# Retention heads: the decay moved onto v and into the group norm's epsilon, two transposes per unit

## The reference, cut to what matters

```python
decay = where(rel >= 0, exp(rel * log_gamma), 0)          # rel = i - j inside a chunk
xi    = exp((pos + 1) * log_gamma);  zeta = exp((c - 1 - pos) * log_gamma)
inner = einsum('bnihd,bnjhd->bnhij', qc, kc) * decay      # scores of a chunk
inner = einsum('bnhij,bnjhe->bnihe', inner, vc)
new_state = einsum('bjhd,bjhe->bhde', k_i * zeta, v_i) + chunk_decay * state
cross = einsum('bnihd,nbhde->bnihe', qc, prev_states) * xi
o = inner + cross
o = (o - mean(o)) * rsqrt(var(o) + 1e-6)                  # over the 64 of a head
return silu(g) * (o * gn_w + gn_b)
```

## Time and profile before

| | |
|---|---|
| time, median of 3 runs (lowest, highest) | 2803.08 us (2801.38, 2803.82) |
| the profiled execution's own time | 2803.51 us |
| its span in the profile | 2801.7 us |
| PE busy, share of the span | 2616.1 us, 93% |
| DVE, ACT, POOL busy | 1545.0, 1106.1, 1043.1 us |
| first layer: retention loop to the projection's first matmul | 565.0 to 660.1 us |
| second layer: the same | 1950.8 to 2046.7 us |

### The profile page before, as it was taken

How to read it: one execution, slowest core, us unless ns; L and a number is a source line. 1 busy time by engine, 2 the same in 40 slices (tenths; PEclk the granted TensorE clock), 3 DMA queues, 4 the chain that set the end, 5 groups by cost and what they waited for, 6 DMA issues and landing times. The chain is left out here.

```text
span 2801.7 us, 43296 instructions
## 1 busy us (share of the span) xinstructions
PE 2616.1 (93%) x13164; PEld 2250.8 (80%) x13164; DVE 1545.0 (55%) x2993; ACT 1106.1 (39%) x2567; POOL 1043.1 (37%) x1271
## 2 busy tenths in 40 slices
PE   6999888989999999999989997988898999999997
PEld 5999777867778888888879996777787888888886
DVE  4666453373464555477657765433725544544785
ACT  4444453262432222244444444433515323223444
POOL 3454422173144444301034554221911554452012
PEclk9999999958999999999989999998599999999999
DMA  5110101021323332473331101012122223335633
GB/s 172 28 57 19 40 5 36 29 91 60 102 72 109 105 109 89 149 291 99 99 105 31 34 19 37 6 36 71 49 83 79 94 94 109 109 105 198 234 98 121
DMA packets 238653, 243.09 MB, mean 87 GB/s; under 512 B 27904, under 2 KB 170752, under 8 KB 238464
## 3 DMA queue, kind: packets, MB, share of 16 engines
q1 hardware_dynamic: 238464, 240.83, 26.5%
HBM read 173.14 MB, written 67.63 MB: 86 GB/s over the span
## 5 line engine op out<-in xcount | busy, mean ns | idle before, releaser
L2256 POOL TENSOR_TENSOR fw_a_lo<-fw_a_raw,fw_a_hi 128x512 fp32r<-128x512 f32 x132 | 179.2, 1358 | 527.2 <-DVE fw_s_raw L1859 527.2
L2256 POOL TENSOR_TENSOR fw_s_lo<-fw_s_raw,fw_s_hi 128x512 fp32r<-128x512 f32 x176 | 230.0, 1319 | 50.8 <-ACT fw_s_hi L1377 50.8
L693 PE MATMUL banks<-ht_hi,da_hi 128*128 128x512 f32 x496 | 192.9, 389 | 0.0
L693 PE MATMUL banks<-ht_lo,da_hi 128*128 128x512 f32 x496 | 192.9, 389 | 0.0
L693 PE MATMUL banks<-ht_hi,da_lo 128*128 128x512 f32 x496 | 192.9, 389 | 0.0
L693 PE MATMUL banks<-w_diff_hi,ht_hi 128*128 128x384 f32 x512 | 180.3, 352 | 6.4 <-DVE ht_lo L1563 4.4
L1193 ACT ACTIVATE pt_hi<-banks 128x512 fp32r<-128x512 f32 (+2 forms) x144 | 67.4, 502 | 298.1 <-PE banks L796 297.9
L693 PE MATMUL banks<-w_diff_hi,ht_lo 128*128 128x384 f32 x512 | 172.4, 337 | 0.0
L693 PE MATMUL banks<-w_diff_lo,ht_hi 128*128 128x384 f32 x512 | 172.1, 336 | 0.0
L2104 POOL TENSOR_TENSOR qk_rot<-rope_a,rope_b 128x512 f32<-128x512 f32 x64 | 82.7, 1293 | 208.2 <-DVE rope_b L1592 208.2
L1620 DVE TENSOR_REDUCE stats<-banks 128x1 f32<-128x1024 f32 (+3 forms) x192 | 138.8, 749 | 38.0 <-PE banks L890 33.0
(11 more groups left out here) (354 smaller groups left out, 7781.2 us busy)
## 6 DMA issues: line engine op xcount, KB each, us to landing
da_raw<-act_scratch SPq DMA_DIRECT2D x154, 256.0 KB, 2.6
fw_a_raw<-in_w_gate_dram SPq DMA_DIRECT2D x88, 256.0 KB, 3.0
act_scratch<-act_s SPq DMA_DIRECT2D x66, 256.0 KB, 3.0
w_diff_raw<-in_w_in_dram SPq DMA_DIRECT2D x24, 512.0 KB, 5.8
fw_a<-in_w_up_dram SPq DMA_DIRECT2D x44, 256.0 KB, 3.2
fw_a_raw<-in_w_up_dram SPq DMA_DIRECT2D x44, 256.0 KB, 2.9
act_scratch<-act_zero SPq DMA_DIRECT2D x44, 256.0 KB, 2.4
act_scratch<-act_one SPq DMA_DIRECT2D x44, 256.0 KB, 2.8
```

The lines of the kernel that those rows point to most:

```text
L693: mm = pe.matmul(bank, lhsT, rhs, start=first and i == 0, stop=last and i == len(pairs) - 1, skip_group_check=resumes)
L2256: pool.tensor_tensor(w[1][:], w[2][:], w[0][:].bitcast(F32), ALU.subtract).then_inc(S["f_lo"], 1)
```

## The change

In a chunk, the decay between output row i and column j is gamma^(i+1) times gamma^-(j+1). The column factor gamma^-(j+1), with the scale of 64^-0.5, is now multiplied onto v, by one more DVE instruction before each rotation. The row factor gamma^(i+1) is left out: it scales a whole row of the output, and the group norm takes it out again if its epsilon is multiplied by gamma^(-2(i+1)), a table of two columns per pair. So:

- the scores are multiplied by a triangle of ones and zeros, 128x128, instead of the `decay` table of 128x512; its DMA carries 64 KB instead of 256 KB;
- neither q nor k is scaled: `ret_scaled` (four ACT instructions per unit) and the third transpose go, and `rt_hi` and `rt_lo` are 256 wide instead of 384;
- the state is multiplied by the chunk's decay when it is rounded: ACT with a scale, and the low part by a DVE scalar_tensor_tensor (`ret_state_low`) instead of POOL's subtraction;
- the normalisation goes from DVE to ACT (`ret_normed`, two instructions Identity with scale and bias), and DVE only forms the bias `r_nb` (`ret_offset`);
- POOL adds the epsilon from the table, a tensor_tensor instead of a tensor_scalar;
- on ACT `rt_hi` stands ahead of `rk_hi`, and the loop runs two steps further for the last two `ret_normed`, ahead of `weights(CH_OUT + 1)`.

```diff
+    age = (pos[:, None] + 1.0) * log_gamma[None, :].astype(np.float64)
     for p in range(RET_PAIRS):
-        c[:, C_XZ + 4 * p:C_XZ + 4 * p + 2] = xi[:, 2 * p:2 * p + 2]
-        c[:, C_XZ + 4 * p + 2:C_XZ + 4 * p + 4] = zeta[:, 2 * p:2 * p + 2]
+        c[:, C_XZ + 4 * p:C_XZ + 4 * p + 2] = (np.exp(-age) * RET_DIM ** -0.5)[:, 2 * p:2 * p + 2]
+        c[:, C_XZ + 4 * p + 2:C_XZ + 4 * p + 4] = (GN_EPS * np.exp(-2.0 * age))[:, 2 * p:2 * p + 2]
...
-                arrives(decay[:], decay_dram.rearrange("p (a n) -> p a n", a=RET_PAIRS), "ret_in")
+                arrives(causal[:], causal_dram, "ret_in")
...
-                    pe.wait_ge(S["r_xz"], L * PER["r_xz"] + n + 1)
+                    pe.wait_ge(S["rope_sum"], L * PER["rope_sum"] + ROPE_RET + n + 1)
...
-                    pe.transpose(bank[:, tokens(2)], r_xzt[n % 3][:, 0:2, :].rearrange("p a d -> p (a d)"), ident[:])\
...
-                    for i in range(4):
-                        st = act.activation(r_xzt[n % 3][:, i, :], r_rot[n][:, i, :], ACT.Copy, scale=xz[:, n // T, i:i + 1])
...
+                def ret_normed(n):
+                    b = n % 2
+                    act.wait_ge(S["r_nb"], L * PER["r_nb"] + n + 1)
...
+                    for j in range(2):
+                        st = act.activation(r_norm[b][:, 64 * j:64 * j + 64], r_sum[b][:, j, :], ACT.Identity,
+                                            bias=r_nb[:, b, j:j + 1], scale=r_rs[:, b, j:j + 1])
...
-                for n in range(1, RET_UNITS + 2):
+                for n in range(1, RET_UNITS + 4):
                     if 1 <= n <= RET_UNITS:
+                        ret_high(n - 1)
                         ret_high_k(n - 1)
-                        ret_high(n - 1)
-                    if n >= 2:
+                    if 2 <= n < RET_UNITS + 2:
                         ret_inner(n - 2)
+                    if n >= 4:
+                        ret_normed(n - 4)
                     if n + 1 < RET_UNITS:
                         ret_gate_and_v(n + 1)
-                        ret_scaled(n + 1)
                     if 2 <= n < 2 + PARTS:
                         weights(CH_OUT, [n - 2])
                 weights(CH_OUT + 1)
...
+                    v = r_z[n][:, 2 * P:3 * P].rearrange("p (j d) -> p j d", j=2)
+                    dve.tensor_tensor(v, v, xz[:, n // T, 0:2].unsqueeze(2).to_broadcast([P, 2, RET_DIM]), ALU.mult)
                     rotate(r_z[n][:, 0:2 * P], r_ab[0], r_ab[1], n % T).then_inc(S["rope_ab"], 1)
...
+                def ret_state_low(n):
...
+                        dve.scalar_tensor_tensor(r_st2[i % 3][:, 1, :], r_st[:], cd[:, p:p + 1], r_st2[i % 3][:, 0, :].bitcast(F32),
+                                                 ALU.mult, ALU.subtract).then_inc(S["r_stlo"], 1)
...
+                def ret_offset(n):
...
+                    dve.scalar_tensor_tensor(r_nb[:, b, :], mv[:, b, :, 0], -1.0, r_rs[:, b, :], ALU.mult, ALU.mult).then_inc(S["r_nb"], 1)
```

More of the change, by code:

```diff
@@ L359, in hybrid_block_kernel @@
     sin_m = keep("sin_m", [P, T, 2, 16])
-    stats = keep("stats", [P, 148])
+    stats = keep("stats", [P, 152])
     taken = [0]
@@ L401, in hybrid_block_kernel @@
     r_ms = small(2, 2)
+    r_nb = small(2, 2)
     minus_half = small(4)
-    assert taken[0] <= 148, taken[0]
+    assert taken[0] <= 152, taken[0]
     assert base + at[0] <= nc.sbuf_usable_end, at[0] - CREG
@@ L1319, in ret_high @@
                         act.wait_ge(S["ro_done"], L * PER["ro_done"] + n - 2)
-                    act.activation(rt_hi[n % 3][:].rearrange("p b n -> p (b n)"), banks[:, TR_BANKS[r % 2], 0:3 * P], ACT.Copy)\
+                    act.activation(rt_hi[n % 3][:].rearrange("p b n -> p (b n)"), banks[:, TR_BANKS[r % 2], 0:2 * P], ACT.Copy)\
                         .then_inc(S["tr_hi"], 1)
@@ L1776, in ret_inner @@
                         dve.wait_ge(S["r_atlo"], L * PER["r_atlo"] + n)
-                    dve.tensor_tensor(r_at[:].rearrange("p (j n) -> p j n", j=2), banks[:, 0:2, 0:P], decay[:, p, :].rearrange("p (j n) -> p j n", j=2), ALU.mult).then_inc(S["r_at"], 1)
+                    dve.tensor_tensor(r_at[:].rearrange("p (j n) -> p j n", j=2), banks[:, 0:2, 0:P], causal[:].unsqueeze(1).to_broadcast([P, 2, P]), ALU.mult).then_inc(S["r_at"], 1)
                     if n % T < T - 1:
@@ L1811, in ret_normed @@
                     if n >= 2:
-                        dve.wait_ge(S["r_gw"], L * PER["r_gw"] + n - 1)
-                    for j in range(2):
-                        st = dve.tensor_scalar(r_norm[b][:, 64 * j:64 * j + 64], r_sum[b][:, j, :],
-                                               mv[:, b, j, 0:1], r_rs[:, b, j:j + 1], ALU.subtract, ALU.mult)
-                    st.then_inc(S["r_on"], 1)
+                        dve.wait_ge(S["r_on"], L * PER["r_on"] + n - 1)
+                    dve.scalar_tensor_tensor(r_nb[:, b, :], mv[:, b, :, 0], -1.0, r_rs[:, b, :], ALU.mult, ALU.mult).then_inc(S["r_nb"], 1)
                 for a in MLA_STEPS:
@@ L2204, in ret_low_k @@
                     pool.wait_ge(S["r_kzhi"], L * PER["r_kzhi"] + n + 1)
-                    pool.tensor_tensor(rk_lo[b][:], r_xzt[n % 3][:, 2:4, :].rearrange("p a d -> p (a d)"), rk_hi[b][:].bitcast(F32), ALU.subtract)\
+                    pool.tensor_tensor(rk_lo[b][:], r_rot[n][:, 2:4, :].rearrange("p a d -> p (a d)"), rk_hi[b][:].bitcast(F32), ALU.subtract)\
                         .then_inc(S["r_kzlo"], 1)
@@ L2220, in ret_root @@
                     pool.sem_inc(S["passed"], 1)
-                    pool.tensor_scalar(r_ms[:, b, :], mv[:, b, :, 1], GN_EPS, None, ALU.add).then_inc(S["r_ms"], 1)
+                    pool.tensor_tensor(r_ms[:, b, :], mv[:, b, :, 1], xz[:, n // T, 2:4], ALU.add).then_inc(S["r_ms"], 1)
                     pool.wait_ge(S["r_ms"], L * PER["r_ms"] + n + 1)
```

62 lines of the change are left out of this document (25 added, 37 removed).

## The result

| | before | changed |
|---|---|---|
| time, median | 2803.45 us | 2823.74 us (2822.96 to 2825.42) |
| span of the profiled execution | 2801.7 us | 2823.6 us |
| first `r_at` to first `ht_lo`, first layer | 77.29 us | 85.91 us |
| the same, second layer | 77.29 us | 85.93 us |

The ratio is 1.0071, with a 95% interval of 1.0057 to 1.0084: 20.3 us slower. The forecast was +6.7, and 2816 as the upper end of its range. The direction was right, the size a third of what came. The ratios in this document leave out one slow execution, of e5 (4904.45 us, one of ten).

The account below looks back on a forecast made before the run. The retention was taken to have no single bound but five stretches with different last waits; -0.3 - 1.5 + 4.7 + 0.2 + 0.25 = +3.35 us a layer, twice +6.7, gave 2809.8 us, range 2803 to 2816.

Parts of the forecast that it names:

- The start: First r_at, waiting for gn_b's DMA: the smaller table ahead of it gains 0.3 us a layer, between 0 and 1.2.
- The steps with w_o: Retention steps with POOL's four w_o_lo: later starts 6.2 us apart instead of 6.47, 1.5 us a layer gained (0.3 to 2.5).
- rival 1: DVE's scalar_tensor_tensor is not held by POOL, so r_nb goes through at once: net +1.5 a layer, 2806; chance 0.18.
- Rival 3: In the steps with w_o, ACT's waiting r_norm holds rt_hi and scores: steps stay 6.47, no gain, 2813; chance 0.09.
- The later units: Units after the w_o steps: one transpose less on PE, 0.9 us a layer gained of a possible 1.7 (0.2 to 1.7).
- The ring: Root, r_nb, r_norm on ACT, three products, epsilon, root: 3.9 us, or 4.2 with the next low part in the way.
- The last units: Units 14 and 15: two more turns through ACT at 0.3 each, 0.6 us a layer lost (0.4 to 1.2).
- From the last root to `ht_lo`: Retention's end: w_o's four ACT roundings now stand behind the last r_norm, 4.7 us a layer lost (4.5 to 5.0).
- Clock and MLA steps: PE's idle before the refill costs 0.2 us a layer (0 to 2.5); the product on v costs 0.25 at the last rotation.
- rival 2: TensorE's clock does not come back while PE refills its banks: 1.6 us a layer more, 2813; chance 0.12.
- Rival 4: PE's clock rises to 2.4 GHz inside the loop: 6.5 us a layer faster, 2790; chance 0.06.
- The chances: Probabilities given for the measured outcome: slower 0.56, same 0.38, faster 0.06, with about 0.2% as the limit.

Follow-up runs that it names:

- e5: Changed kernel with DVE's sum and statistics of unit n-3 moved ahead of v's and the state's low parts, ACT's order untouched; 2803.5 us, ratio 0.9995.
- e1: Changed kernel with v's copy and the gate of unit n+1 ahead of the normalisation of unit n-4 on ACT; 2808.5 us, ratio 1.0011.
- e3: Changed kernel with the normalisation back as two DVE instructions, no r_nb, ACT's loop two steps shorter; 2796.9 us, ratio 0.9966.
- e4: Changed kernel with v's copy and gate ahead of the normalisation, and w_o's second half rounded in pairs after units 13 and 14; 2798.2 us, ratio 0.9973.
- e7: Changed kernel with the normalisation back on DVE, and DVE's sum and statistics ahead of v's and the state's low parts; 2791.0 us, ratio 0.9942.
- e2: Changed kernel with w_o's second half rounded on ACT in two pairs, behind the normalisations of units 13 and 14; 2816.5 us, ratio 1.0041.
- e8: Kernel before with only DVE's sum and statistics of unit n-3 moved ahead of v's low part; 2804.9 us, ratio 0.9998.

## Why the prediction was off, step by step

- **The start**, -0.3: the first `r_at` came 6.82 and 6.70 us after the last `m_sum` instead of 7.82 and 8.86; over all kernels it comes 1.3 us earlier on the mean with the smaller table, a little beyond the bound of 1.2. `gn_b` landed after 4.6 and 4.2 us (4.7 and 5.9 before). Mis-sized.
- **The steps with w_o**, -1.5: here the prediction failed. The first two `w_o_lo` started 2.59 after `r_at` and 5.20 later, as forecast (2.45, 5.1). The next two came every 6.78, not 6.2, and the fourth 21.35 after `r_at` instead of 19.95: 0.15 gained and not 1.5. The step that failed is "I take 6.2, between 6.02 and the 6.47 of before": it made POOL's own queue and 6.47 the ends of the range. 6.02 was a good value of POOL's queue (e1: 6.00), and DVE was held as the prediction had it (`r_nb` 2.30 behind `w_o_lo`, 0.41 beside other work, 0.16 alone), so rival 1 is out. But nothing made 6.47 an upper end. Rival 3 had the mechanism half, `r_norm` at the head of ACT's queue with work behind it, and priced it at a gain of 0; it named `rt_hi` and the scores as what waits, not v's copy. From the fourth `w_o_lo` to unit 7's `r_at`, for which the sum has no term, the same ring took 1.55 us more.
- **The later units**, -0.9: the second place where it failed. The ring was drawn from the root through `r_norm` to POOL's three products, 3.9 us. That ring exists and is not the last one; the one through ACT's next instruction and DVE's queue is 4.73. The eight units lost 1.8 us instead of gaining 0.9. At the end the prediction followed what is queued on ACT behind the moved instructions; in the loop it did not. PE's side of the term was right. Full units went from 4.56 to 4.35 wherever the ring through ACT is open (e1, e3, e4, e5, e7), and unit 7's transposes to unit 15's from 34.7 to between 32.8 and 33.2, where 1.7 less was worked out.
- **The last units**, -0.6 for the ring through ACT: the last two roots were 3.52 apart, 3.27 before, so 0.25 a turn, and 0.3 was taken. Right; the pair of `r_norm` took 0.68 to the next issue and not 0.48.
- **From the last root to `ht_lo`**, +4.7: 6.00 instead of 1.20, +4.80 in both layers. Right in size and cause (e2, e4).
- **Clock and MLA steps**, +0.2 and +0.25: the clock came back during the refill (0.56 in the window from 666 us, 1.00 in the next), so rival 2 is out, and the projection came 10.6 and 11.0 us after `ht_lo` instead of 11.1 and 10.8. The product on v costs under 0.1. That the clock might fall elsewhere, in unchanged code, by several us either way, was in neither the sum nor the range, though one profiled execution was taken as the base of a sum of 6.7 us. That left 5.6 of the 20.3 us without a term.
- **Rival 4**, the clock rising in the loop: it stayed at 0.50 in every kernel here.
- **The chances**: those of the cases add up to 0.57 for slower and 0.37 for the same, not 0.56 and 0.38.

## What to carry to other kernels

When an instruction that waits is put into an in-order queue, take each instruction behind it, even one that has nothing to do with it, and follow it to the other engines until a path closes: the length of that closed path is the new unit, whatever the engines' loads say. Work without a late input (here v's copy) belongs ahead of work with one, and of two orders the one that sets the ring's next value first wins (e5, e7). What an order is worth depends on which engine goes without a wait: the same move on DVE brought 0.7 us a layer where POOL already ran without a gap in the steps with w_o (e8) and 3.1 where POOL still waited there (e7 against e3). Ask this for each stretch by itself: behind those steps it is PE that runs without a wait.

## What the runs showed of the hardware that was not expected

- TensorE's clock falls behind the same wait of 1.5 us in one execution and not in another. The MLA steps of the changed program took 185.9 to 188.7 us; with the clock's part taken off, all 26 stretches of all kernels lie within 1.5 us (177.3 to 178.8). A difference of a few us between two profiles says nothing until the clock's windows have been laid side by side.
- On ACT, an Identity on 128x64 with scale and bias from memory takes 434 ns, a pair 0.68 us to the next issue; the Copy with a scale alone takes 333 ns, four pieces 1.05 us.
- POOL's tensor_tensor on 128x2 (`ms` plus the table's epsilon) took 190 ns, less than the tensor_scalar's 221 that it replaced; the root's 0.71 was no measure for it.
- DVE's scalar_tensor_tensor on 128x2, 0.16 us alone, took 2.30 while POOL's 2.35 us `w_o_lo` ran. The Trainium skill, "SBUF — State Buffer", section "Who interferes with whom", says that a DVE instruction with two SBUF inputs and a GpSimd one that reads SBUF exclude each other; here the trace agrees. That the state's low part would still be in POOL's way on DVE, so that the steps stay at 6.2, did not follow: e1 makes them in 6.00, with POOL never idle.
